# Three transformer layers on one core: other byte positions for the slots of rounded weights and for all tensors behind them

## What is computed

```python
# first block, two times
h = rmsnorm(x, norm_mix[l])
q, k, v, u, ug, ga, gb = split(h @ w_in[l])
a_out = sliding_window_attention(q, k, v, sinks[l])
c_out = conformer_conv(u, ug, ..., w_conv_out[l])
x = x + (sigmoid(ga) * a_out + sigmoid(gb) * c_out) @ w_out[l]
g, up = split(rmsnorm(x, norm_ffn[l]) @ w_gate_up[l])      # 1024 -> 2 * 2816
x = x + (silu(g) * up) @ w_down[l]                          # 2816 -> 1024
# second block, once
z, xbc, dt, q, k, v = split(modulated_norm(x) @ w_in_2)
x = x + g1 * (concat(ssd(...), stick_breaking(q, k, v)) @ w_out_2)
x = x + g2 * ((silu(h @ w_gate_2) * (h @ w_up_2)) @ w_down_2)
```

## The kernel before, in words

| tensor | before | after |
|---|---|---|
| `hh`, `hl`, `raw` | 128 | 128 |
| `wh`, slots 0 to 3 | 128, 128, 128, 128 | 128, 192, 256, 320 |
| `wl`, slots 0 to 3 | 128, 128, 128, 128 | 384, 448, 0, 64 |
| `tmp`, constants | 128 | 128 |
| `ah`, `al`, `mh`, `ml`, `ssd_h`, `ssd_l`, `oh`, `ol`, `ch` | 448 | 480 |
| `cl` | 416 | 448 |

## Time and profile before

### The profile page before, as it was taken

How to read it: one execution, slowest core, us unless ns; L and a number is a source line. 1 busy time by engine, 2 the same in 40 slices (tenths; PEclk the granted TensorE clock), 3 DMA queues, 4 the chain that set the end, 5 groups by cost and what they waited for, 6 DMA issues and landing times.

```text
span 2182.7 us, 28930 instructions
## 1 busy us (share of the span) xinstructions
PE 2171.3 (99%) x10369; PEld 1751.4 (80%) x10369; DVE 1197.7 (55%) x1584; ACT 937.9 (43%) x1505; POOL 1062.9 (49%) x527
## 2 busy tenths in 40 slices
PE   9999999999999999999999999999999999999999
PEld 7877788888888887788888888887786678888887
DVE  7877854222436887874222345859877746333201
ACT  5556633222214556633333215336645655444311
POOL 4963334444544883244444443433766754444442
PEclk9999999999999999999999999999999999999999
DMA  5332223333662332232333572322231012333332
GB/s 181 105 92 68 68 88 98 97 97 97 211 216 87 107 99 61 68 96 88 96 97 96 184 239 77 106 77 68 68 92 54 30 50 86 106 96 96 96 96 87
DMA packets 62869, 219.57 MB, mean 101 GB/s; under 512 B 7936, under 2 KB 8192, under 8 KB 62784
## 3 DMA queue, kind: packets, MB, share of 16 engines
q1 hardware_dynamic: 55296, 191.16, 28.9%
q10 hardware_dynamic: 7488, 27.27, 3.7%
HBM read 212.76 MB, written 2.10 MB: 98 GB/s over the span
## 4 chain that ended last, share of the span: by engine, by line
PE 91%; DVE 4%; POOL 2%; issue 2%; ACT 1%; POOLq 0%; DVEq 0%
PE bank L1725 28%; PE bank L1727 28%; PE bank L1726 28%; PE bank L1905 1%; PE bank L1931 1%; PE bank L1965 1%; POOL soft_lo L497 1%; PE bank L1799 1%; DVE soft_hi L1618 1%; POOL wl L406 0%; PE bank L1939 0%; PE bank L1812 0%; DVE tmp L1543 0%; DVE bank L1030 0%; DVE tmp L1619 0%
## 5 line engine op out<-in xcount | busy, mean ns | idle before, releaser
L406 POOL TENSOR_TENSOR wl<-raw,wh 128x1024 fp32r<-128x1024 f32 x349 | 855.2, 2452 | 1008.5 <-ACT wh L553 1008.5
L1725 PE MATMUL bank<-hh,wh 128*128 128x512 f32 (+1 forms) x1979 | 773.0, 391 | 0.8 <-DVE hl L1425 0.6
L1727 PE MATMUL bank<-hh,wl 128*128 128x512 f32 (+1 forms) x1979 | 763.9, 386 | 0.0
L1726 PE MATMUL bank<-hl,wh 128*128 128x512 f32 (+1 forms) x1979 | 763.1, 386 | 0.0
L553 ACT ACTIVATE wh<-raw 128x1024 fp32r<-128x1024 f32 x351 | 370.0, 1055 | 592.6 <-PE bank L1727 544.3
L1725 PEld LDWEIGHTS bank<-hh,wh 128*128 128x128 f32 x1979 | 372.1, 188 | 77.5 <-issue 3.7
L1727 PEld LDWEIGHTS bank<-hh,wl 128*128 128x128 f32 x1979 | 372.0, 188 | 75.2
L1726 PEld LDWEIGHTS bank<-hl,wh 128*128 128x128 f32 x1979 | 372.3, 188 | 74.3 <-issue 1.7
L1725 PE MATMUL bank<-ah,wh 128*128 (+1 forms) x512 | 201.9, 394 | 0.0
L1727 PE MATMUL bank<-ah,wl 128*128 (+1 forms) x512 | 200.8, 392 | 0.0
L1726 PE MATMUL bank<-al,wh 128*128 (+1 forms) x512 | 198.9, 388 | 0.0
(11 more groups left out here) (383 smaller groups left out, 2753.0 us busy)
## 6 DMA issues: line engine op xcount, KB each, us to landing
raw<-stream SPq DMA_DIRECT2D x351, 512.0 KB, 3.6
ada_w<-ada ACTq DMA_DIRECT2D x48, 512.0 KB, 4.6
x<-x_t ACTq DMA_DIRECT2D x4, 512.0 KB, 7.6
out_t<-x SPq DMA_DIRECT2D x8, 256.0 KB, 2.1
th<-q SPq DMA_DIRECT2D x16, 64.0 KB
th<-q SPq DMA_DIRECT2D x64, 16.0 KB
q<-th SPq DMA_DIRECT2D x16, 64.0 KB, 2.0
cst<-consts SPq DMA_DIRECT2D x1, 640.0 KB, 6.4
```

Of the source, the lines that this page charges most:

```text
L406: nc.gpsimd.tensor_tensor(wl[:, slot, :], raw[:, raw_slot, :], wh[:, slot, :].bitcast(F32), ALU.subtract).then_inc(lo_ready, 1)
L1725: mm(dst, wh[:, slot, w], xh, start=start, stop=False)
L1726: mm(dst, wh[:, slot, w], xl, start=False, stop=False)
L1727: return mm(dst, wl[:, slot, w], xh, start=False, stop=stop)
```

## The change

Each slot of `wh` and of `wl` becomes 16 float32 (64 bytes) longer, and those 16 are never used. So slots of one tensor start 64 bytes apart by the rest of 512, and `wl` starts 4 x 64 = 256 bytes further than before, against `wh`. A new tensor of 8 float32 (32 bytes) that nothing uses lies ahead of `den`; it moves everything behind it by 32 bytes by the rest of 512 (the 512 bytes that the eight longer slots take together change no rest). The reserve at the start goes from 16384 to 8192 bytes, which makes room and changes no rest by 512. Three instructions name the used 1024 columns of a slot in place of the whole slot. No instruction is added, removed or put elsewhere on any engine, and no wait is changed.

```diff
-        wh, wl = sb("wh", [P, RW, D], F32R), sb("wl", [P, RW, D], F32R)
+        wh, wl = sb("wh", [P, RW, D + 16], F32R), sb("wl", [P, RW, D + 16], F32R)
...
         touched = row_max[:, 1, 0:1]
+        sb("line_up", [P, 8])
         den, sink_exp, rden = sb("den", [P, 2, 4]), sb("sink_exp", [P, 2, 4]), sb("rden", [P, 2, 4])
...
-                nc.gpsimd.tensor_tensor(wl[:, slot, :], raw[:, raw_slot, :], wh[:, slot, :].bitcast(F32),
+                nc.gpsimd.tensor_tensor(wl[:, slot, 0:D], raw[:, raw_slot, :], wh[:, slot, 0:D].bitcast(F32),
...
-                af(wh[:, slot, :], raw[:, raw_slot, :], ACT.Copy).then_inc(hi_ready, 1)
+                af(wh[:, slot, 0:D], raw[:, raw_slot, :], ACT.Copy).then_inc(hi_ready, 1)
...
-                tt(wl[:, c, :], raw[:, c, :], wh[:, c, :].bitcast(F32), ALU.subtract).then_inc(lo_ready, 1)
+                tt(wl[:, c, 0:D], raw[:, c, :], wh[:, c, 0:D].bitcast(F32), ALU.subtract).then_inc(lo_ready, 1)
...
-    nc = bacc.Bacc("TRN2", target_bir_lowering=False, num_devices=1)
+    nc = bacc.Bacc("TRN2", target_bir_lowering=False, num_devices=1, dynamic_dma_scratch_size=8192)
```

## The result

The changed kernel takes 2213.43 us (median of two runs, 2212.75 and 2214.10), against 2184.74 before: ratio 1.0131, 95% interval 1.0115 to 1.0147. That is 28.7 us more; 18.7 more had been forecast.

A forecast was written before the change was run, and what follows sets the result against it. The prediction took TensorE's matmul pace to bound the kernel. Its terms, 13.4 us for `hh` and 5.3 for inner values, sum to 18.7 us more on 2184.5, making 2203 us, range 2152 to 2234.

The forecast's parts named there:

- What bounds the kernel: TensorE, busy 2171.3 of 2182.7 us: time is the number of matmuls times their pace, plus a few short waits.
- rounding and rests would stay hidden: ScalarE and GpSimd slot writers: even a tenth slower, 3.9 us of a chunk's 5.4 us or more; nothing taken.
- `hh` against the slots: 1995 threes with `hh` meeting spread weight slots: 6.7 ns more each, 13.4 us more; bounds 58 less, 80 more.
- Inner values: 772 threes with `ah`, `mh`, `ssd_h`, `oh`, moved 32 bytes off: 6.9 ns more each, 5.3 us more.
- the `ch` threes: 64 threes with one operand 32 off before, another after: nothing, bounds 3 us less and 2 us more.
- The bound from above: Longest start distance in a steady stream, 240 ns, 720 a three: 80 us more for `hh`, 26 for inner values.
- Bad distances: Rival: with eight distances in turn the stream never settles; 2293 us, with half of them 2239; chance 0.12.
- Addresses don't matter: Rival: the three paces come from something else and the change does nothing; 2184.7 us, plus or minus 2; chance 0.22.
- Equal rests are the conflict: Rival: stream and weights meet at equal rests, spreading ends it; 2108 us, with half the gain 2146; chance 0.22.
- the kernel could not get below 216 ns: Floor for a matmul of 512 columns, from the skill's gap rule N / 2.4 + 2.5 ns, without the load beside it.

The follow-up runs named there:

- the map: Against the slots-only spread kernel, `wl` brought back to the rest of `wh`, so each slot has one distance (inner values at 448); 2206.74 us in one run.
- the kernel with 16-byte steps: Slots 16 bytes apart instead of the 64 of the 64-byte spread, with `wh` and `wl` at the same rest; 2207.49 us in one run.
- the kernel with 8-byte steps: Slots 8 bytes apart instead of the 64 of the 64-byte spread, with `wh` and `wl` at the same rest; 2207.69 us in one run.

## Why the prediction was right, and where it was off

*What bounds the kernel.* Right: the 28 us are in the pace of the matmuls with weights, none in waits or writers. The step that rounding and rests would stay hidden held; they did not even get slower.

*`hh` against the slots.* The mechanism was right, and this term was mis-sized: 13.4 us forecast, 18.8 measured. It took the one row at another distance, 192 away, which is 6.7 ns more for a three, for all others. In the map that distance is the mildest of the coarse ones (multiples of 64 other than 0). The four slots average (5.45 + 5.60 + 5.57 + 5.51) / 4 = 5.53 us, 0.09 more for a tile, 11.6 ns for a three. Over all 1995 threes it was 18.8 / 1995 = 9.4 ns. The 153 tiles that ran undisturbed before paid 14.7 of the 18.8 us, 12.0 ns for a three; the other threes paid less, and those with 256 columns, which I counted whole, nothing (30.8 us before, 30.6 after). I counted by the rest of 512, and the runs repeat every 256; that changed no number, since one price was used for all distances. My counts also leave out 29 threes with 256 columns (5 with `hh`, 8 with `ah`, 16 with `oh`), which is 0.2 us at the prices I used.

*Inner values.* Same kind of miss: 5.3 us forecast, 9.7 measured (7.0, 1.6 and 1.1). The price was taken from the stretch with `ch` and `cl`, in which only `cl` is 32 bytes off: its 693.6 ns for a three mix the distance 224 with 192. All by itself a distance of 160 gives 5.600 us a tile, 700 ns for a three, which is 13 more than 686.7 where I took 6.9. The reason behind this term, that 32 bytes off cost more than whole steps of 64, does not hold: the distance 64 takes 5.600 us a tile too. The sign came out right because the inner values left 192, the mildest of the coarse distances, and that is luck. For the `ch` threes themselves I forecast nothing, and it was 0.4 us less.

*The bound from above.* The 240 ns of the earlier trace rows are a difference of two rounded starts. In ns they are 265.442 and 265.675, so 233, and the longest distance from 262.90 to 268.45 is 237. The bound and the rival "Bad distances" were reckoned a little too high by it; the forecast doesn't use it.

*The rivals.* "Addresses don't matter" is excluded by the two runs that moved one side alone, 23 and 9 us more. "Equal rests are the conflict" is the reverse of what holds: equal rests are the best of all distances tried, and making them equal everywhere is what gained 0.26%. "Bad distances" had the idea of a stream that never settles, and in fact 0 is the distance at which it settles at the lowest pace; but the price was at most 5.62 us a tile, 234 ns a matmul. Single distances of 240 and 241 ns do occur in the changed kernel, in the tiles at distance 128, which average 232.

*The Trainium skill.* The page "SBUF — State Buffer", section "Who interferes with whom", has TensorE's two reads independent and waiting on nobody. The runs are not with it: the same instructions at a granted clock of 1.00 take 5.44 to 5.62 us a tile when nothing but the addresses of the two operands changes. What it says of 16-byte lines doesn't cover this either, since steps of 64 bytes matter and 256 don't. From the page "TensorE: Matmul & The Clock Gate", section "Back-to-back issue gap", I took that the kernel could not get below 216 ns. That doesn't follow from the page: the same section says that the formula over-counts for a stream of loads and matmuls with 512 columns, and gives 131 ns. No stretch here is near that: the lowest steady pace is 226.7 ns in float32 and 217 in bf16.

*What stays open.* Why equal rests are best. That the load of the weights and the stream beside it meet in memory fits the dependence on their distance, but no run took the load away, so it is not shown. The 10 ns that remain above the bf16 pace at distance 0 were not touched by any kernel. A load beside the stream is not enough to explain them, since the bf16 matmuls have one each too (10369 loads for 10369 matmuls). Why the same distance can have two paces (last section) is open as well. Distances that are not in the table were not tried.

## What to carry to other kernels

When TensorE is at 99%, look at the distance from one start to the next and not at durations, and compare stages that ought to be alike: 226.7 against 228.9 ns was the whole clue here. Put the stationary and the moving operand of a stream of such matmuls (float32 rounded for the matmul, 128 x 128 weights, 512 columns) at the same start by the rest of 256 bytes, and keep the slots of a ring a multiple of 256 bytes apart. Spreading them, as one might against a conflict, cost 1.05% here, and 1.3% with the inner values moved too. A pad in front of a group of tensors is enough to test it.

## What the runs showed that I had not expected

The pace depends on what came before, not on the distance alone. At 16 bytes the stream keeps 5.45 us a tile when it comes from a slot at distance 0 (the kernel with 16-byte steps), and takes 5.60 when it comes from one at 8 (the kernel with 8-byte steps), except for one tile there, right behind matmuls with 256 columns, which took 5.45. At 192 bytes there are two paces as well. In the changed kernel most undisturbed tiles of slot 3 with `hh` (33 of 40) take 5.51 us, but four take 5.60 (at 72.9, 99.6, 749.0 and 775.8 us, each behind a tile that was interrupted at its start); in the kernel with 8-byte steps three tiles at 192 take 5.60 and the others 5.49 to 5.50. At 240 bytes tiles of 5.46 and of 5.50 us alternate in one kernel. At distance 0 the first few matmuls of a tile take 227 to 236 ns after another slot, and then 226.7 each. So the table is a guide to what a layout costs and no law.

The other distances settle too, but into cycles: at 192 the starts are 226, 229 and 232 ns apart in turn, at 64 they are 231 and 236 in the changed kernel and 233 to 234 in the one with the inner values at 64, with the same mean, and at 24 they are 229 and 231. Within a stage a tile repeats to within 0.002 us in nearly all of the distances, 5.440 again and again in three layers. So differences of a tenth of a per cent in a tile can be read from a single profile, though not from a single time: the runs of before lie between 2184.27 and 2186.03 us.
